# Three of the eight input tiles transposed on VectorE, by way of DRAM, during the convolution's first unit

## The chip, the cores and the metric
The kernel runs on one core of a Trainium2 chip. The metric is the time on the device of one execution, in microseconds (us). The core has five engines with a queue of instructions each: TensorE (PE, products and transposes through its array), VectorE (DVE), ScalarE (ACT), GpSimd (POOL) and SyncE (SP, which here only issues transfers). They run side by side and are tied together by semaphores: an instruction waits until a counter has reached a value and adds to a counter when it is done.

## What is computed
One decoder block on x of 1024 tokens by 1024 channels, in float32. The part that matters here is its beginning:

```python
h = rmsnorm(x, g_mix[i])
z = h @ w_in[i]                       # 1024 x 1536
a = z[..., :C_CONV]; b = z[..., C_CONV:2 * C_CONV]; v = z[..., 2 * C_CONV:]
u = a * jax.nn.sigmoid(b)
u = causal_depthwise_conv(u, conv_w[i], conv_b[i])      # 31 taps, 512 channels
u = jax.nn.silu(layernorm(u, ln_g[i], ln_b[i]))
q = multiscale_pool(v, pool_w[i], pool_scale[i])
x = x + jnp.concatenate([u, q], axis=-1) @ w_out[i]
# then a SwiGLU FFN, a gated per-token embedding and a final rmsnorm
```

## The kernel before
**Precision and tiles.** Each float32 operand of a product is split into a rounded high part and a low part (hi and lo); one product is three matmuls (lo x hi, hi x lo, hi x hi: L1659 to L1661). ScalarE writes the high part (`copy`, L1042), VectorE or GpSimd the low part as source minus high part (`lo`, L2035 and L788). Tokens lie in eight tiles of 128 (t = 0 to 7), channels in eight blocks of 128 (k).

**The input side.** For each tile: SP loads x into `xres[:, t]` (the tile `resid`), ScalarE sums its squares (`square_x`), GpSimd makes the factor (`rms`), VectorE multiplies by it and by the gain (`normed`, L2063) into one of two slots of `scr`, TensorE transposes the 8 blocks of 128x128 into two banks of PSUM (`turn`, L1708), ScalarE copies them to `act_hi` (`turned_hi`) and VectorE makes `act_lo` from them (`turned_lo`), in two halves each.

**The products.** TensorE computes a and b in eight products n = 0 to 7, ordered by `AB`: n = 0 to 3 are the channel groups for tokens 0 to 511, n = 4 to 7 those for tokens 512 to 1023. Each is two halves (a, then b) of 24 matmuls of 128x512, in two banks of PSUM: 0 and 1 for even n, 2 and 3 for odd n. Product 0 is done in pieces while the first tiles come in. Product 1 needs weight stripes 2 and 3 (`ws_lo`), products 2 and 3 those of `bs_hi` and `bs_lo`: stripes 0 and 1, whose low parts VectorE makes, and 2 and 3, whose low parts GpSimd makes. Products 4 to 7 need `act_lo` of all eight tiles. Tiles 4 and 5 are transposed between the pieces of product 0, 6 and 7 between the halves of product 1. `evac_ab` on ScalarE moves a product out, GpSimd multiplies by the gate (`gate_u`).

**The convolution.** It runs on VectorE in eight units of 31 taps (`convolve`, L2129), one for each group of 128 channels and half of the tokens. The first `OWN` taps of a unit are made by ScalarE (`first_taps`, L1094) and summed by GpSimd (`sum_taps`), 2 in units 0 and 7. VectorE's first two taps of a unit read two operands in SBUF, the later ones accumulate in PSUM. `between` names steps that are set in after a tap of a given number: in unit 1 the two transposes of p (`turn_p`), later layer norm and the low parts of the mixing. GpSimd waits at some places until VectorE has done the first two taps of a unit (`unit_begun`), not for unit 7.

**Behind it.** The v part of the projection, a product for e, the pooled products (each waits for the low part of the one before, `q_low`), the output projection for each tile, and a second norm whose tiles 0 to 4 already go the way that the change takes: stored to DRAM, loaded in runs of 32 elements, transposed on VectorE (`store_xn`, `load_xn`, `block_turn`, L2215). The latter needs the end of unit 7, because the same queue of VectorE holds the additions (`add_x`, L2181) behind it.

**What sets the order.** It is written by hand: each engine's program is a list of calls, and an engine never passes one that waits. DMA queues go in the order in which SP issues them.

Of the kernel before, what the change touches and what calls it, by code (L numbers as in the profile page):

```python
# [39 lines left out]
def hybrid_block(nc, x, p, g_mix, w_in, conv_w, conv_b, ln_g, ln_b, pool_w, pool_scale, w_out,  # L40
# [34 lines left out]
    xg_dram = nc.dram_tensor("xg_scratch", (TT, 2, P, BANK), F32, kind="Internal").ap()  # L75
    x1_dram = nc.dram_tensor("x1_scratch", (TT, P, D), F32, kind="Internal").ap()
    in_dram = nc.dram_tensor("in_scratch", (7, PAIRS, P, BANK), F32, kind="Internal").ap()

    with ExitStack() as ctx:
# [79 lines left out]
        def turns(n):  # L159

            by_dve = sum(TT <= k < TT + MIX_TILES or 0 <= k - 2 * TT and k - 2 * TT in DVE_TURNS for k in range(n))
            return 2 * (n - by_dve)

        DVE_TURNS = (0, 1, 2, 4, 6)

# [48 lines left out]
        xn_turned = sem("xn_turned")  # L214
        w_hi = sem("w_hi")
# [125 lines left out]
        def turn_bank(norm, t):  # L341

            return (6 - 2 * (t % 2), 4 * (t % 2), 2 if t % 2 == 0 else 0 if t == 1 else 4)[norm]
# [199 lines left out]
        def _(sp):  # L543
# [234 lines left out]
        def _(pool):  # L778
# [261 lines left out]
        def _(act):  # L1040
# [86 lines left out]
            turned_hi(4, 0)  # L1127
            turned_hi(5, 0)
# [527 lines left out]
        def _(pe):  # L1656
# [30 lines left out]
            def turn(t, norm):  # L1687
                n = norm * TT + t
                for j in range(2):
# [67 lines left out]
            turn(4, 0)  # L1757
            turn(5, 0)
# [9 lines left out]
            for n in range(1, 2 * KC):  # L1768
# [33 lines left out]
            for s in range(GROUPS):  # L1802
                pe.wait_ge(w_lo, S_V + s + 1)
# [35 lines left out]
            pe.wait_ge(w_lo, S_PLE + KP)  # L1839
# [779 lines left out]
```

## Time and profile before

| | |
|---|---|
| Time, median of 3 runs | 992.76 us (992.42 to 993.64) |
| Profiled execution: its own time | 994.86 us |
| Profiled execution: its span | 992.9 us |
| TensorE busy | 980.3 us (99%) |
| VectorE busy | 710.7 us (72%) |
| ScalarE busy | 458.1 us (46%) |
| GpSimd busy | 380.4 us (38%) |
| Clock granted to TensorE | 0.998 of full, on average |

The span is the time from the first to the last instruction in one profiled execution; the times are of executions without the profiler. The matmuls' ends are modelled, so small waits of TensorE are seen better in the distance between starts than in its busy time. Of two engines that are busy at once only the one on which the other waits counts for the end.

### The profile page before, as it was taken

The page shows a single profiled execution, that of the slowest core. Times are in us where ns is not written, and L with a number is a line of the kernel's source. Part 1 is how long each engine was busy: PE and PEld are TensorE (multiplying, and loading weights), DVE is VectorE, ACT ScalarE, POOL GpSimd, SP SyncE. Part 2 cuts the span into 40 slices and gives each one's busy share as a digit, 9 for nine tenths or more (in the row PEclk, how much of TensorE's full clock was granted, in tenths as well). Part 3 has the DMA queues.
Part 4 walks back from the last instruction along what each step waited for, and adds up shares of the span by engine and source line. Part 5 has one row for each costly group of instructions (what it writes and reads, how often), then busy time and mean ns, then how long its engine had stood idle before and what let it go on. Part 6 is the DMA issues. An engine that isn't in the chain of part 4 may idle for free.

```text
span 992.9 us, 12311 instructions
## 1 busy us (share of the span) xinstructions
PE 980.3 (99%) x4447; PEld 812.3 (82%) x4447; DVE 710.7 (72%) x982; ACT 458.1 (46%) x704; POOL 380.4 (38%) x288
## 2 busy tenths in 40 slices
PE   9999999999999999999999999999999999999996
PEld 7888888888788888888888888888888888888885
DVE  6899999996798355354454544553677888887897
ACT  7625347404363333423333333333444665676865
POOL 3445889710245544444354353442000000012555
PEclk9999999999999999999999999999999999999999
DMA  7620112558724234233332432412999788657432
GB/s 257 140 87 40 45 41 116 202 172 190 211 64 153 60 109 121 89 107 95 117 107 80 133 107 64 148 64 99 355 370 322 233 304 268 198 159 201 152 107 106
DMA packets 154799, 148.74 MB, mean 150 GB/s; under 512 B 56507, under 2 KB 110291, under 8 KB 154739
## 3 DMA queue, kind: packets, MB, share of 16 engines
q1 hardware_dynamic: 153536, 147.56, 46.7%
q8 instruction: 35, 0.57, 0.2%
q10 hardware_dynamic: 1202, 0.40, 0.2%
q14 instruction: 26, 0.20, 0.1%
HBM read 109.92 MB, written 38.01 MB: 149 GB/s over the span
## 4 chain that ended last, share of the span: by engine, by line
PE 70%; DVE 2%; DMA 2%; SPq 1%; issue 1%; POOL 1%; ACT 1%; POOLq 0%; DVEq 0%; ACTq 0%
PE ps L1659 23%; PE ps L1661 23%; PE ps L1660 23%; SPq L627 1%; DMA xn_scratch<-scr 1%; DMA scr<-xn_scratch 1%; PE ps L1708 0%; DVE resid L2181 0%; DVE scr L2063 0%; DVE ftmp L2522 0%; POOL rs L785 0%; DVE resid L2525 0%; DVE act_lo L2035 0%; SPq L632 0%; ACT junk L1056 0%
## 5 line engine op out<-in xcount | busy, mean ns | idle before, releaser
L782 POOL TENSOR_SCALAR ss<-ss 128x1 f32<-128x1 f32 x38 | 14.5, 381 | 322.0 <-ACT junk L1056 286.6
L2129 DVE SCALAR_TENSOR_TENSOR ps<-resid,convw,ps 128x512 f32<-128x512 f32 x190 | 127.4, 749 | 0.0
L1659 PE MATMUL ps<-ring_hi,ring_lo 128*128 128x512 f32 x308 | 119.9, 389 | 0.1
L1661 PE MATMUL ps<-ring_hi 128*128 128x512 f32 x308 | 119.8, 389 | 0.0
L1660 PE MATMUL ps<-ring_lo,ring_hi 128*128 128x512 f32 x308 | 119.8, 389 | 0.0
L1659 PE MATMUL ps<-act_hi,bs_lo 128*128 128x512 f32 x240 | 93.5, 389 | 0.0
L1660 PE MATMUL ps<-act_lo,bs_hi 128*128 128x512 f32 x240 | 93.4, 389 | 0.0
L1661 PE MATMUL ps<-act_hi,bs_hi 128*128 128x512 f32 x240 | 93.4, 389 | 0.0
L2288 DVE TENSOR_TENSOR gtmp<-ps,gtmp 128x512 f32<-128x512 f32 x22 | 15.2, 691 | 95.6 <-PE ps L1661 95.6
L1042 ACT ACTIVATE ring_hi<-raw 128x512 fp32r<-128x512 f32 x89 | 51.9, 625 | 60.5 <-PE ps L1661 58.1
L2035 DVE TENSOR_TENSOR ring_lo<-raw,ring_hi 128x512 fp32r<-128x512 f32 x89 | 58.0, 688 | 22.9 <-ACT ring_hi L1042 22.8
L788 POOL TENSOR_TENSOR wc_lo<-raw_b,wc_hi 128x1024 fp32r<-128x1024 f32 x22 | 55.6, 2525 | 48.9 <-ACT wc_hi L1042 47.8
L1659 PEld LDWEIGHTS ps<-ring_hi,ring_lo 128*128 128x128 f32 x308 | 57.8, 188 | 12.3 <-DVE ring_lo L2035 0.5
L1661 PEld LDWEIGHTS ps<-ring_hi 128*128 128x128 f32 x308 | 57.8, 188 | 12.1
L1660 PEld LDWEIGHTS ps<-ring_lo,ring_hi 128*128 128x128 f32 x308 | 57.8, 188 | 12.0
L788 POOL TENSOR_TENSOR bs_lo<-raw_b,bs_hi 128x1024 fp32r<-128x1024 f32 x24 | 58.0, 2417 | 23.0 <-ACT bs_hi L1042 14.7
L788 POOL TENSOR_TENSOR bs_lo<-raw,bs_hi 128x1024 fp32r<-128x1024 f32 x17 | 41.1, 2425 | 62.6 <-ACT bs_hi L1042 62.6
L1659 PE MATMUL ps<-act_hi,ws_lo 128*128 128x512 f32 (+1 forms) x144 | 53.5, 372 | 0.3 <-DVE act_lo L2035 0.2
L1659 PEld LDWEIGHTS ps<-act_hi,bs_lo 128*128 128x128 f32 x240 | 45.1, 188 | 9.4
L1661 PEld LDWEIGHTS ps<-act_hi,bs_hi 128*128 128x128 f32 x240 | 45.1, 188 | 9.4
L1661 PE MATMUL ps<-act_hi,ws_hi 128*128 128x512 f32 (+1 forms) x144 | 52.7, 366 | 0.0
L1660 PE MATMUL ps<-act_lo,ws_hi 128*128 128x512 f32 (+1 forms) x144 | 52.7, 366 | 0.0
(281 smaller groups left out, 2620.7 us busy)
## 6 DMA issues: line engine op xcount, KB each, us to landing
raw<-in_w_gate_up SPq DMA_DIRECT2D x44, 512.0 KB, 5.2
raw<-in_scratch SPq DMA_DIRECT2D x52, 256.0 KB, 3.3
raw<-in_w_down SPq DMA_DIRECT2D x52, 256.0 KB, 4.2
in_scratch<-in_s SPq DMA_DIRECT2D x44, 256.0 KB, 3.4
in_scratch<-gtmp SPq DMA_DIRECT2D x33, 256.0 KB, 2.3
keep<-in_w_down SPq DMA_DIRECT2D x32, 256.0 KB, 4.1
keep<-in_scratch SPq DMA_DIRECT2D x25, 256.0 KB, 3.6
resid<-in_x SPq DMA_DIRECT2D x8, 512.0 KB, 6.9
```

The lines of the kernel that those rows point to most:

```text
L627: sp.dma_start(xn_place(TT + t)[a * SQ:(a + 1) * SQ, :].rearrange("j (k b i) -> j k b i", k=KD, i=SQ), src)\
L782: pool.tensor_scalar(ss[:, n:n + 1], ss[:, n:n + 1], 1.0 / D, EPS, ALU.mult, ALU.add)\
L788: pool.tensor_tensor(dst, src, hi.bitcast(F32), ALU.subtract).then_inc(done, 1)
L1042: act.activation(dst, src, ACT.Copy, scale=scale).then_inc(done, 1)
L1659: pe.matmul(dst, w_lo_, m_hi, start=start, stop=False, skip_group_check=onto)
L1660: pe.matmul(dst, w_hi_, m_lo, start=False, stop=False, skip_group_check=onto)
L1661: return pe.matmul(dst, w_hi_, m_hi, start=False, stop=stop, skip_group_check=onto)
L2035: dve.tensor_tensor(dst, src, hi.bitcast(F32), ALU.subtract).then_inc(done, 1)
L2129: dve.scalar_tensor_tensor(out=conv_c if k == last_odd else acc, in0=u_all[:, c, k + h * BANK:k + (h + 1) * BANK], scalar=convw[:, c * 32 ...
L2288: dve.tensor_tensor(gtmp[:, 3, :], ps[:, X_BANK[q % 2], :], gtmp[:, 3, :], ALU.add).then_inc(c22_ok, 1)
```

## The change
**Which tiles.** Tiles 4, 5 and 6 (`X_DVE`) are normed in place, into `xres[:, t]` and not into `scr`. SP stores each to DRAM (`xa_scratch`, `store_xa`) and loads it again with four DMAs (`load_xa`), each for 32 partitions and in runs of 32 elements, so that the 32x32 blocks stand where a transposition by blocks needs them. VectorE then transposes the 128x1024 in one instruction into banks 6 and 7 (`x_turn`). Tile 7 is still transposed by TensorE, between the halves of product 1, now into banks 0 and 1, which product 2 uses next. `act_hi` and `act_lo` are made as before, in the order of tiles 7, 4, 5, 6 (`x_place`).

**What moves.** TensorE loses 24 transposes. The three block transposes, four `turned_lo` and the low part of stripe 1 of bs are set in between the taps of units 0 and 1. ScalarE makes the first taps of unit 0 before it copies stripe 1. GpSimd does the first two v stripes before those for e, so TensorE's counts of `w_lo` change with it. The stores and loads come ahead of the loads of p in SP's queue.

The diff, in the order SP, GpSimd, ScalarE, TensorE, VectorE behind the tables of numbers:

```diff
         def turns(n):
-            by_dve = sum(TT <= k < TT + MIX_TILES or 0 <= k - 2 * TT and k - 2 * TT in DVE_TURNS for k in range(n))
+            by_dve = sum(k in X_DVE or TT <= k < TT + MIX_TILES or 0 <= k - 2 * TT and k - 2 * TT in DVE_TURNS for k in range(n))
...
+        X_DVE = (4, 5, 6)
+        def x_place(t):
+            return t if t < 4 else 4 if t == 7 else t + 1
...
         def turn_bank(norm, t):
-            return (6 - 2 * (t % 2), 4 * (t % 2), 2 if t % 2 == 0 else 0 if t == 1 else 4)[norm]
+            return ((6, 4, 6, 4, 6, 6, 6, 0)[t], 4 * (t % 2), 2 if t % 2 == 0 else 0 if t == 1 else 4)[norm]
...
+            def store_xa(t):
+                sp.wait_ge(xn_ok, t + 1)
+                sp.dma_start(xa_dram[t - 4], x_tile(t, 0)).then_inc(xa_moved[t - 4], DMA)
+            def load_xa(t):
+                sp.wait_ge(xa_moved[t - 4], DMA)
+                for a in range(P // SQ):
+                    src = xa_dram[t - 4].rearrange("(b j) (k a i) -> a j k b i", j=SQ, a=P // SQ, i=SQ)[a]
+                    sp.dma_start(x_tile(t, 0)[a * SQ:(a + 1) * SQ, :].rearrange("j (k b i) -> j k b i", k=KD, i=SQ), src)\
+                      .then_inc(xa_moved[t - 4], DMA)
...
             unit_begun(3)
-            for r in range(KP):
-                split_row(raw_b, r, bs_hi[:, 2 + r, :], bs_lo[:, 2 + r, :], S_PLE + r + 1)
             gate_u(6)
             for s in range(2):
                 split_cols(V_STRIPE[s], S_V + s + 1, at=s)
+            split_row(raw_b, 0, bs_hi[:, 2, :], bs_lo[:, 2, :], S_PLE + 1)
+            gate_u(7)
             sum_taps(KC)
-            gate_u(7)
+            split_row(raw_b, 1, bs_hi[:, 3, :], bs_lo[:, 3, :], S_PLE + 2)
...
-            turned_hi(4, 0)
-            turned_hi(5, 0)
             square_x(6)
             square_x(7)
             evac_ab(0)
-            for m in range(2):
-                split_cols(m, 2 * DMA, bs_hi)
-            turned_hi(6, 0)
+            split_cols(0, 2 * DMA, bs_hi)
+            first_taps(0)
+            split_cols(1, 2 * DMA, bs_hi)
             turned_hi(7, 0)
-            first_taps(0)
             evac_ab(1)
...
+            turned_hi(4, 0)
             first_taps(1)
+            turned_hi(5, 0)
             evac_ab(2)
+            turned_hi(6, 0)
...
-            turn(4, 0)
-            turn(5, 0)
...
+                if n == 2:
+                    pe.wait_ge(act_lo_ok, 2 * x_place(7) + 2)
                 if n == KC:
                     pe.wait_ge(act_lo_ok, 2 * TT)
                 ab_part(n, 0)
                 if n == 1:
-                    turn(6, 0)
                     turn(7, 0)
...
-            turned_lo(4, 0)
-            turned_lo(5, 0)
             normed(6, 0, 1)
             normed(7, 0, 1)
...
+            def x_turn(t):
+                dve.wait_ge(xa_moved[t - 4], DMA * (1 + P // SQ))
+                dve.wait_ge(act_lo_ok, 2 * x_place(t))
+                dve.transpose(ps[:, 6:8, :].rearrange("p b n -> p (b n)"), x_tile(t, 0)).then_inc(xa_turned, 1)
+            b_stripe_low(0)
+            dve.wait_ge(act_lo_ok, 2 * HT)
...
-            convolve(0, {})
-            convolve(1, {8: lambda: turn_p(0), 16: lambda: turn_p(1)})
+            convolve(0, {2: lambda: b_stripe_low(1), 4: lambda: turned_lo(7, 0), 8: lambda: x_turn(4),
+                         12: lambda: turned_lo(4, 0), 16: lambda: x_turn(5), 20: lambda: turned_lo(5, 0),
+                         25: lambda: x_turn(6)})
+            convolve(1, {0: lambda: turned_lo(6, 0), 8: lambda: turn_p(0), 16: lambda: turn_p(1)})
```

VectorE's queue from the constants (`qscale`) to unit 0, before. The rows L2035 are `act_lo` of tiles 4 and 5, then two stripes of `bs_lo`, then `act_lo` of 6 and 7; L2129 are taps.

```order
L2035 TENSOR_TENSOR act_lo<-ps,act_hi 128x4x128 [waits act_hi_ok] x4
L2063 SCALAR_TENSOR_TENSOR scr<-resid,rs,gain 128x1024 [waits turned,rs_ok] x2
L2035 TENSOR_TENSOR bs_lo<-raw,bs_hi 128x1024 [waits w_hi] x2
L2035 TENSOR_TENSOR act_lo<-ps,act_hi 128x4x128 [waits act_hi_ok] x4
L2129 SCALAR_TENSOR_TENSOR ps<-resid,convw,gain 128x512 [waits taps_in,act_lo_ok]
L2129 SCALAR_TENSOR_TENSOR ps<-resid,convw,gain 128x512
L2129 SCALAR_TENSOR_TENSOR ps<-resid,convw,ps 128x512 [waits taps_done] x25
```

The same place now (the lines are 31 to 35 further down): L2094 are the norms of tiles 6 and 7, L2164 taps, L2140 the transpose of tile 4.

```order
L2094 SCALAR_TENSOR_TENSOR resid<-resid,rs,gain 128x1024 [waits rs_ok]
L2094 SCALAR_TENSOR_TENSOR scr<-resid,rs,gain 128x1024 [waits turned,rs_ok]
L2066 TENSOR_TENSOR bs_lo<-raw,bs_hi 128x1024 [waits w_hi]
L2164 SCALAR_TENSOR_TENSOR ps<-resid,convw,gain 128x512 [waits taps_in,act_lo_ok]
L2164 SCALAR_TENSOR_TENSOR ps<-resid,convw,gain 128x512
L2164 SCALAR_TENSOR_TENSOR ps<-resid,convw,ps 128x512 [waits taps_done]
L2066 TENSOR_TENSOR bs_lo<-raw,bs_hi 128x1024 [waits w_hi]
L2164 SCALAR_TENSOR_TENSOR ps<-resid,convw,ps 128x512 [waits taps_done] x2
L2066 TENSOR_TENSOR act_lo<-ps,act_hi 128x4x128 [waits act_hi_ok] x2
L2164 SCALAR_TENSOR_TENSOR ps<-resid,convw,ps 128x512 [waits taps_done] x4
L2140 STREAM_TRANSPOSE ps<-resid 128x1024 [waits act_lo_ok,xa_moved0]
L2164 SCALAR_TENSOR_TENSOR ps<-resid,convw,ps 128x512 [waits taps_done] x4
```

Everything that came between the norms and the taps but the first stripe now stands behind taps; four taps on there follow `act_lo` of tile 4, the transpose of 5, and so on.

SP's queue from the last weights of product 1 to p, before: L550 are stripes of w_in, L587 the loads of p.

```order
L562 DMA resid<-in_x 128x1024 x2
L550 DMA raw<-in_w_in 128x8x256 [waits w_lo]
L550 DMA raw<-in_w_in 128x8x256
L587 DMA raw_b<-in_p 32x32x32 x8
L589 DMA pw_raw<-in_pool_w 128x4x128
```

And now: L594 are the stores, L600 the loads of tiles 4, 5 and 6, L614 those of p.

```order
L571 DMA resid<-in_x 128x1024 x2
L594 DMA xa_scratch<-resid 128x1024 [waits xn_ok] x2
L559 DMA raw<-in_w_in 128x8x256 [waits w_lo]
L559 DMA raw<-in_w_in 128x8x256
L600 DMA resid<-xa_scratch 32x32x32 [waits xa_moved0]
L600 DMA resid<-xa_scratch 32x32x32 x3
L594 DMA xa_scratch<-resid 128x1024 [waits xn_ok]
L600 DMA resid<-xa_scratch 32x32x32 [waits xa_moved1]
L600 DMA resid<-xa_scratch 32x32x32 x3
L600 DMA resid<-xa_scratch 32x32x32 [waits xa_moved2]
L600 DMA resid<-xa_scratch 32x32x32 x3
L614 DMA raw_b<-in_p 32x32x32 x8
```

Two stores stand ahead of the stripes, a third store and twelve loads between them and p.

## Rows read from the trace of the kernel before
In a timeline a row is: start us, us in all, engine, line, operation, output <- inputs, shape, how many in a row, and in brackets the idle time before it and what ended it. In the view of a line: duration in ns (min/median/max), first and last start in us; then the time from a DMA's issue to its landing.

**Rows 1.** Timeline, TensorE, around its waits at 250, 261 and 271 us.
```profile
249.49 0.39 PE L1661 MATMUL ps<-bs_hi,act_hi 128*128 128x512 f32 x1
250.02 0.50 PE L1659 MATMUL ps<-bs_hi,act_lo 128*128 128x512 f32 x1
...
260.81 0.39 PE L1661 MATMUL ps<-ws_hi,act_hi 128*128 128x512 f32 x1
261.25 1.09 PE L1708 MATMUL ps<-ident,scr 128*128 128x128 f32 x8
...
270.14 0.39 PE L1661 MATMUL ps<-bs_hi,act_hi 128*128 128x512 f32 x1
271.49 1.09 PE L1708 MATMUL ps<-ident,scr 128*128 128x128 f32 x8 [0.95 <-DVE scr L2063]
```

**Rows 2.** Timeline, TensorE: transposes of tiles 4 and 5; what follows; start of product 2.
```profile
22.68 1.91 PE L1708 MATMUL ps<-ident,scr 128*128 128x128 f32 x16
24.52 0.43 PE L1763 MATMUL ps<-ident,scr 31*128 31x31 f32 x4
...
40.58 0.39 PE L1659 MATMUL ps<-act_hi,bs_lo 128*128 128x512 f32 x1
```

**Rows 3.** Timeline, VectorE, 31 to 65 us: low parts, unit 0, start of unit 1.
```profile
31.98 1.23 DVE L2035 TENSOR_TENSOR bs_lo<-raw,bs_hi 128x1024 fp32r<-128x1024 f32 x1 [0.87 <-ACT bs_hi L1042]
35.36 1.23 DVE L2035 TENSOR_TENSOR bs_lo<-raw,bs_hi 128x1024 fp32r<-128x1024 f32 x1 [2.16 <-ACT bs_hi L1042]
36.51 2.48 DVE L2035 TENSOR_TENSOR act_lo<-ps,act_hi 128x512 fp32r<-128x512 f32 x4
39.02 1.43 DVE L2129 SCALAR_TENSOR_TENSOR ps<-resid,convw,gain 128x512 f32<-128x512 f32 x2
40.35 16.55 DVE L2129 SCALAR_TENSOR_TENSOR ps<-resid,convw,ps 128x512 f32<-128x512 f32 x25
...
59.05 1.42 DVE L2129 SCALAR_TENSOR_TENSOR ps<-resid,convw,gain 128x512 f32<-128x512 f32 x2
...
64.99 1.24 DVE L2195 STREAM_TRANSPOSE wide<-raw_b 128x1024 f32<-128x1024 f32 x1
```

**Rows 4.** Timeline, ScalarE: copy of stripe 1, first taps, evacuation of product 3.
```profile
34.27 1.06 ACT L1042 ACTIVATE bs_hi<-raw 128x1024 fp32r<-128x1024 f32 x1 [2.33 <-DMA raw<-in_w_in]
...
37.14 0.83 ACT L1094 ACTIVATE gain<-resid,cvec,convw 128x512 f32<-128x512 f32 x1
37.85 0.73 ACT L1094 ACTIVATE gain<-resid,convw 128x512 f32<-128x512 f32 x1
...
62.54 0.60 ACT L1077 ACTIVATE resid<-ps 128x512 f32<-128x512 f32 x1 [9.79 <-PE ps L1661]
```

**Rows 5.** View of line L587, the loads of p: all eight, and the last.
```profile
L587 SPq DMA_DIRECT2D raw_b<-in_p x8: 563/970/3202, 26.7 to 38.0; - x8
...
L587 SPq DMA_DIRECT2D raw_b<-in_p x1: 902/902/902, 38.0 to 38.0; - x1
...
DMA to landing us min/median/max: 4.5/4.5/4.5
```

**Rows 6.** Timeline, VectorE and GpSimd, first steps of unit 6.
```profile
160.82 1.29 DVE L2035 TENSOR_TENSOR act_lo<-ps,act_hi 128x512 fp32r<-128x512 f32 x2 [0.61 <-ACT act_hi L1042]
...
169.50 1.28 DVE L2169 SCALAR_TENSOR_TENSOR act_lo<-ps,qscale,act_hi 128x1024 fp32r<-128x1024 f32 x1 [0.80 <-ACT act_hi L1042]
...
160.38 2.41 POOL L903 TENSOR_TENSOR scr<-wide,scr 128x1024 f32<-128x1024 f32 x1 [1.78 <-DVE ps L2129]
```

**Rows 7.** Timeline, VectorE and GpSimd, first taps of unit 7.
```profile
186.31 5.59 DVE L2129 SCALAR_TENSOR_TENSOR ps<-resid,convw,gain 128x512 f32<-128x512 f32 x2
...
186.14 5.20 POOL L788 TENSOR_TENSOR bs_lo<-raw,bs_hi 128x1024 fp32r<-128x1024 f32 x2 [0.54 <-ACT bs_hi L1042]
```

**Rows 8.** Timeline, VectorE, 226 to 230 us.
```profile
226.39 0.69 DVE L2181 TENSOR_TENSOR resid<-ps,raw_b 128x512 f32<-128x512 f32 x1 [0.98 <-PE ps L1661]
229.00 1.25 DVE L2215 STREAM_TRANSPOSE raw<-scr 128x1024 f32<-128x1024 f32 x1 [1.92 <-DMA scr<-xn_scratch]
```

More of the change, by code:

```diff
@@ L75, in hybrid_block @@
     xg_dram = nc.dram_tensor("xg_scratch", (TT, 2, P, BANK), F32, kind="Internal").ap()
+    xa_dram = nc.dram_tensor("xa_scratch", (3, P, D), F32, kind="Internal").ap()
     x1_dram = nc.dram_tensor("x1_scratch", (TT, P, D), F32, kind="Internal").ap()
@@ L214, in hybrid_block @@
         xn_turned = sem("xn_turned")
+        xa_moved = [sem(f"xa_moved{j}") for j in range(3)]
+        xa_turned = sem("xa_turned")
         w_hi = sem("w_hi")
@@ L581, in _ @@
             load_x(7, xres[:, 7, :])
+            def store_xa(t):
[7 more added lines that the diff above has]
+                      .then_inc(xa_moved[t - 4], DMA)
+            store_xa(4)
+            store_xa(5)
             sp.wait_ge(w_lo, S_B)
             load_cols(w_in_v, 256, C + 256)
+            load_xa(4)
+            store_xa(6)
+            load_xa(5)
+            load_xa(6)
             for k in range(KP):
@@ L1060, in turned_hi @@
                 for j in range(2):
-                    act.wait_ge(turned, 2 * n + j + 1)
+                    if n in X_DVE:
+                        act.wait_ge(xa_turned, X_DVE.index(n) + 1)
+                    else:
+                        act.wait_ge(turned, turns(n) + j + 1)
                     copy(act_hi[:, 4 * j:4 * j + 4, t * P:(t + 1) * P],
@@ L1693, in turn @@
                         pe.wait_ge(xn_ok, n + 1)
-                    if norm == 0 and t >= 2:
+                    if norm == 0 and 2 <= t < 4:
                         pe.wait_ge(act_lo_ok, 2 * n + j - 3)
+                    if norm == 0 and t == 7:
+                        pe.wait_ge(ab_ev, 1)
                     if norm == 1 and t >= HT_MIX + 2:
@@ L1802, in _ @@
             for s in range(GROUPS):
-                pe.wait_ge(w_lo, S_V + s + 1)
+                pe.wait_ge(w_lo, S_V + s + 1 - (KP if s < 2 else 0))
                 if s < 2:
@@ L1838, in _ @@
             pe.wait_ge(p_lo_ok, KP)
-            pe.wait_ge(w_lo, S_PLE + KP)
+            pe.wait_ge(w_lo, S_PLE + KP + 2)
             for t in range(TT):
@@ L2037, in turned_lo @@
             def turned_lo(t, norm, halves=range(2)):
-                n = t if norm == 0 else TT + t
+                n = x_place(t) if norm == 0 else TT + t
                 for j in halves:
@@ L2057, in normed @@
                         dve.wait_ge(xn_turned, n - TT - 1)
-                    else:
+                    elif n not in X_DVE:
                         dve.wait_ge(turned, turns(n - 1))
@@ L2062, in normed @@
                         dve.wait_ge(gain_ok, 2)
-                    ins = dve.scalar_tensor_tensor(out=xn_place(n)[:, c], in0=x_tile(t, norm)[:, c], scalar=rs[:, n:n + 1],
+                    ins = dve.scalar_tensor_tensor(out=(x_tile(t, norm) if n in X_DVE else xn_place(n))[:, c], in0=x_tile(t, norm)[:, c], scalar=rs[:, n:n + 1],
                                                    in1=pair(2)[:, c] if n < 5 else gain[:, c],
@@ L2098, in _, with b_stripe_low @@
             ins.then_inc(const_ok, 1)
-            turned_lo(4, 0)
-            turned_lo(5, 0)
             normed(6, 0, 1)
             normed(7, 0, 1)
-            for m in range(2):
+            def b_stripe_low(m):
                 dve.wait_ge(w_hi, S_B + m + 1)
                 lo(cols_stripe(bs_lo, m), cols_of(raw, m), cols_stripe(bs_hi, m), w_lo)
-            turned_lo(6, 0)
-            turned_lo(7, 0)
-            dve.wait_ge(act_lo_ok, 2 * TT)
+            def x_turn(t):
[4 more added lines that the diff above has]
+            dve.wait_ge(act_lo_ok, 2 * HT)
             even, odd = ps[:, 4, :], ps[:, 5, :]
```

## The prediction, made before the change was timed

> **What bounds the kernel now.** I read the page first: TensorE is busy for 980.3 us of 992.9, so only work on TensorE, or a wait of TensorE, can move the end. Then the waits of TensorE: it waits at very few places. The ones near this change lie at 250, 261 and 271 us: the gaps between starts are 0.53, 0.44 and 1.35 us where 0.23 is the rule, so 0.3, 0.2 and 1.1 us, 1.6 in all [rows 1]. Then the timelines of the first 65 us, since the change lies there, and of 155 to 272 us, to see who TensorE waits for later. There TensorE waits for a chain of VectorE and DMA which begins when VectorE ends the eight convolution units. So two clocks matter: how much TensorE moves (call it s) and how much the convolution's end moves (call it c).
>
> **Removed from TensorE.** 24 transposes (tiles 4, 5, 6). Sixteen hold TensorE from 22.68 to 24.52 us, 0.115 each [rows 2], so 24 of them 2.76 us. All of it is on TensorE's path. Without other waits product 2 of the input projection (counted from 0; the first that reads bs_lo) would start at 40.58 - 2.8 = 37.8 us.
>
> **The convolution begins sooner.** What it needs is on ScalarE: the copy of stripe 0 of bs, after which VectorE starts its own part at 31.98 [rows 3], and then the first two taps, which took 37.14 to 38.58 [rows 4], 1.44 us. Now the taps stand right behind stripe 0, so unit 0 starts at about 31.9 + 1.4 = 33.3 us where it was 39.02 [rows 3]. The copy of stripe 0 waits for its transfer, which is issued at the same point as before; the two stores put ahead of it in SP's queue wait only for norms that VectorE has done before the stripe on which that transfer waits, so I take no delay.
>
> **What now stands inside unit 0.** Taps come every 0.66 us (25 in 16.55 us), a bs_lo stripe costs 1.15, one tile's two act_lo halves 2 x 0.63 = 1.25 (four in 2.5) [rows 3], and a VectorE transpose of 128x1024 1.17 (64.99 to the next tap) [rows 3]. In order:
> - three taps to 35.3; stripe 1 of bs_lo needs ScalarE's copy, which waits for its transfer until 34.27 and ends at 35.33 [rows 4]: to 36.5; two taps to 37.8; act_lo of tile 7 to 39.15. **First stall:** product 2 now waits for this one (its bank held tile 7). It starts at 39.2, not 37.8: 1.4 us lost, still 1.4 ahead of before.
> - four taps, transpose of tile 4 (41.7 to 42.9), four taps, act_lo of tile 4, four taps, transpose of tile 5 (49.4), four taps, act_lo of 5, five taps, transpose of 6 (57.8), three taps and the end of the unit. Unit 1 starts at 61.8 (before: 59.05 [rows 3]); one tap, then act_lo of tile 6, done at 63.8.
> - **Second stall:** product 4 needs act_lo of all tiles. Products 2 and 3 took from 40.58 [rows 2] to 62.35 (ScalarE's evacuation at 62.54 [rows 4] follows by 0.2), 21.8 us. So TensorE is ready at 39.2 + 21.8 = 61.0 and waits until 63.85: 2.9 us lost. TensorE is now 1.5 us **later** than before (63.85 against 62.35), and VectorE 4.0 later (61.8 + 1.25 against 59.05).
>
> In sum: removed -2.8, waits +1.4 and +2.9. The three transposes (3.5 us) went from an engine with no slack to one whose result that engine needs, and VectorE's idle time ahead of unit 0, for which they might have been filled in, is still there.
>
> **The transfers.** The new loads have the shape of those of p: 128 KB in runs of 32 elements. Those eight were issued from 26.7 to 38.0 and the last landed 4.5 later, at 42.5 [rows 5], behind two stripes that landed by 34.3 [rows 4]: 1.0 us each. The four of tile 4 take the place of the first four, so they land at 38.4, for a transpose at 41.7: 3.3 us spare. Store 6, tile 5 (44), tile 6 (48 to 49) and then p (57, needed at 69) have more. I take nothing for them; without this cover each us of lateness above the slack costs one.
> The Trainium skill (VectorE: DVE Perf Modes, The three transpose paths) says that a plain DMA that does the transposing by strides is 19 times slower than the crossbar's, and (DMA: Bandwidth & Descriptors, Specifications) that pieces under 512 B miss line rate. That speaks against the change: by it the tiles would come tens of us late. The rows of p show about 4 us for a tile in such runs, and the sum goes by them.
>
> **From there to 190 us.** s = 1.5, VectorE +4.0. Units 1 to 3 have no waits to give back. VectorE's idle 0.61 before act_lo of the mixing (160.82) is used up, and 0.4 ahead of it, so it comes 3.0 late to the first pooled product's low part, and had waited 0.80 there (169.50) [rows 6]: that step ends 2.2 later than before. TensorE waits for it before the next pooled product, so s grows to 2.2. GpSimd waited at 160.38 for unit 6's second tap [rows 6], so its chain comes 3.7 late, ScalarE waits for that and delays the second pooled product's evacuation by 0.6 more: s = 2.8. Bounds: 1.5 if this slack is wider than I read it, 3.3 if ScalarE comes one step later. I take 2.8.
>
> **The end of the convolution.** Unit 7 starts when the last of these products is through: 186.31 + 2.8 = 189.1. Before, its first two taps took 5.59 us and not 1.42, while GpSimd's two bs_lo stripes ran from 186.14 to 191.34 [rows 7]. Each tap was held for one GpSimd instruction, 2.1 us. Now GpSimd starts these stripes about 3.6 later (189.8): the first tap is clear by 0.7 and the second on the edge. So c = 2.8 - 2.1 or 2.8 - 4.2: +0.7 or -1.4.
> (The Trainium skill, SBUF - State Buffer, SBUF: two separate sides, calls this an exclusive lock for a whole instruction between GpSimd and a VectorE instruction with two SBUF inputs. By that rule the price comes in whole steps, where a shared rate would give something between; the row, two taps of about 2.8, agrees with the lock.)
>
> **Where the delay is paid back.** VectorE's addition at 226.39 waited for TensorE [rows 8], so it comes at 229.2; the first block transpose (229.00, it waited for its transfer) then starts at 229.9: the chain moves by 0.9, whichever of the two c holds. At 271.49 TensorE needs that chain at +0.9, and would itself be ready at +2.8 - 1.6 (its old waits [rows 1]) = +1.2. The later counts: **+1.2 us** at 272, and no wait behind it that would absorb or add.
>
> **The sum.** The profiled execution's span is 992.9 us: -2.8 +1.4 +2.9 +1.3 (pooling part) -1.6 (old waits) = +1.2, so 994.1. Its own time was 994.86, above the runs' median of 992.76; I put the difference on the median: **994.0**. A measurement of this kernel tells 0.2% (2.0 us) from no change, so this is "no change".
>
> **Rivals.**
> 1. The pooling part has more slack (s stays about 1.5) and unit 7 is free of GpSimd. Then TensorE is at 1.5 - 1.6, the chain below zero: 992.7. For: three of my links there have less than 0.7 us of margin. Chance 0.15.
> 2. **Slower: both first taps of unit 7 meet GpSimd again.** c = +2.8, all of the chain to 271 moves by it and TensorE waits for it: 995.6. It decides when GpSimd starts the stripes before 189.1, 0.7 sooner than I place it (or unit 7 is 0.7 later). For: it is what happens before. Chance 0.20.
> 3. Slower: the runs of 32 land late. At twice p's 1.0 us the four of tile 4 land at 34.3 + 8.3 = 42.6, 0.9 after their transpose is due; the store of tile 6 takes its turn (1.5, half of a 1 MB stripe's 2.9 to 3.3) and tile 5 lands at 52.4, 2.2 after its own shifted turn; tile 6 is then in time. Product 4 comes 3.1 later still: 997.0. It decides from a tile 4 later than 41.7. Against: the rows of p. Chance 0.06.
> 4. Faster: product 4 is not waited for, because VectorE is quicker or TensorE's need later than I think. Then -2.8, and of the 1.6 of waits up to all: 988.5 to 990.5, say 990. Against: it takes 2.9 us off a row of steps of known length. Chance 0.09.
> My forecast has 0.50.
>
> **Numbers.** Rivals 1 and the forecast lie within 0.2%: 0.65; 2 and 3 are slower: 0.26; 4 is faster: 0.09. Range: from 1 to 2 with the bounds of s and some spread of the runs (992.42 to 993.64): 991.9 to 996.2; 4 and most of 3 are left out.
>
> **What would show it.** TensorE: product 2 at 39.2 and product 4 at 63.8, each after a wait for VectorE's act_lo, 1.4 and 2.9 us; unit 0 starting at 33.3; transposes on VectorE at 41.7, 49.4 and 57.8 with no wait for DMA; unit 1 at 61.8; unit 7 at 189.1 with one long tap or none; the turn before 272 at 272.6. I am wrong if product 4 starts before 62.3, if a transpose waits for its loads, or if unit 7's taps are both long.

## The result, and the profile after

| | us, median | lowest to highest | profiled execution | its span |
|---|---|---|---|---|
| before | 992.87 | 992.42 to 994.18 | 994.86 | 992.9 |
| after | 996.10 | 995.26 to 998.45 | 995.38 | 993.5 |

The ratio after to before is 1.0033, 95% interval 1.0024 to 1.0042: slower, by 3.2 us. The time lies at the upper edge of the range, beyond the forecast of 994.0.

The two profiled spans differ by 0.6 us only, because the profiled execution of before lay 2.1 us above its kernel's median. The first experiment below gives a second profile of it, near the median (992.62, span 990.7), and "before" in what follows is that one. Every trace has its own zero: one and the same piece of product 0 starts anywhere from 19.4 to 20.3 us (19.53 in before, 19.41 in after). I write s for how much later than there TensorE is, and v for the same of VectorE; both hold this difference of zeros unless it is named.

The views that answer to those of before. Waits of TensorE in the changed kernel, whole span (engine, line, waited for: us in total, times, longest):

```profile
PE ps L1689 <- DVE act_lo L2066: 3.7, 4, 2.3
```

Its timeline at the second of these waits, where product 4 starts:

```profile
60.55 0.39 PE L1691 MATMUL ps<-act_hi,bs_hi 128*128 128x512 f32 x1
63.25 0.50 PE L1689 MATMUL ps<-act_hi,bs_lo 128*128 128x512 f32 x1 [2.31 <-DVE act_lo L2066]
63.55 0.62 PE L1690 MATMUL ps<-act_lo,bs_hi 128*128 128x512 f32 x1
63.97 0.63 PE L1691 MATMUL ps<-act_hi,bs_hi 128*128 128x512 f32 x1
...
66.53 0.59 PE L1691 MATMUL ps<-act_hi,bs_hi 128*128 128x512 f32 x1
66.96 0.40 PE L1689 MATMUL ps<-act_hi,bs_lo 128*128 128x512 f32 x1
67.20 0.39 PE L1690 MATMUL ps<-act_lo,bs_hi 128*128 128x512 f32 x1
```

From 63.55 to 66.96 us eight steps are 0.43 us apart; before the wait and after 66.96 they are 0.23 apart. The view of stretches says the same (stretch, its length, busy time and count of PE, PEld, DVE, ACT and POOL, the granted clock, DMA share, GB/s):

```profile
61.00:63.25 2.25, 0.00 (x1) 0.04 (x1) 2.15 (x5) 1.06 (x2) 0.00 (x0) 1.00 0.00 0
63.25:67.00 3.75, 3.75 (x10) 2.93 (x11) 3.75 (x7) 3.20 (x6) 1.29 (x1) 0.54 0.02 4
67.00:75.00 8.00, 8.00 (x37) 6.61 (x36) 8.00 (x13) 0.69 (x2) 4.81 (x2) 1.00 0.00 0
```

The granted clock is 0.54: nearly the whole stretch at the lower level, 1.2 GHz, right after an idle time of 2.3 us. That costs 8 x 0.20 = 1.6 us, and no term of the prediction had it. The Trainium skill (TensorE: Matmul & The Clock Gate, What's actually happening) describes these two levels and says that activity releases the higher one; the rows show both levels, and TensorE at work when the higher one comes back.

VectorE at the steps that replace [rows 3] and [rows 7]: the transposes wait for nothing, `act_lo` of tile 6 stands in unit 1, and both first taps of unit 7 are long again:

```profile
41.30 1.25 DVE L2140 STREAM_TRANSPOSE ps<-resid 128x1024 f32<-128x1024 f32 x1
48.88 1.25 DVE L2140 STREAM_TRANSPOSE ps<-resid 128x1024 f32<-128x1024 f32 x1
57.13 1.25 DVE L2140 STREAM_TRANSPOSE ps<-resid 128x1024 f32<-128x1024 f32 x1
61.15 0.76 DVE L2164 SCALAR_TENSOR_TENSOR ps<-resid,convw,gain 128x512 f32<-128x512 f32 x1
61.82 1.28 DVE L2066 TENSOR_TENSOR act_lo<-ps,act_hi 128x512 fp32r<-128x512 f32 x2
...
115.98 0.69 DVE L2172 TENSOR_TENSOR resid<-ps,resid 128x512 f32<-128x512 f32 x1
...
188.75 5.64 DVE L2164 SCALAR_TENSOR_TENSOR ps<-resid,convw,gain 128x512 f32<-128x512 f32 x2
```

So where did 3.2 us come from? TensorE's first transposes of the convolution's output start at 119.35 us, 116.62 before: s = 2.7 there, and it stays 2.7 through its transposes at 272.11 (269.39 before) to the end (2.8 there: span 993.5 against 990.7). The other 0.4 of the 3.2 us is not in these two traces. All of the loss is made in the first 67 us: -2.7 for the 24 transposes, +1.15 and +2.5 for the two waits, +1.6 for the clock are 2.5 of the 2.7.

### The profile page after: what moved, and what is told of

Read it like the earlier page. It is cut to its first block, busy times and chain, and to the rows that moved or that the text cites. A ratio compares the mean times of both kernels' runs of the same rounds, so it can differ in the third digit from the quotient of the medians.

```text
span 993.5 us, 12276 instructions
## 1 busy us (share of the span) xinstructions
PE 978.8 (99%) x4423; PEld 810.8 (82%) x4423; DVE 713.4 (72%) x985; ACT 458.5 (46%) x704; POOL 382.3 (38%) x288
## 4 chain that ended last, share of the span: by engine, by line
PE 92%; DVE 5%; issue 1%; DMA 1%; ACT 1%; POOL 0%; POOLq 0%; DVEq 0%; ACTq 0%
PE ps L1689 30%; PE ps L1691 30%; PE ps L1690 30%; DVE ps L2164 2%; DVE act_lo L2066 1%; PE ps L1740 1%; DMA raw<-in_w_in 1%; DMA resid<-in_x 0%; DVE ftmp L2559 0%; PE ps L1829 0%; PE ps L1819 0%; DVE ps L2140 0%; DVE ws_lo L2066 0%; DVE resid L2562 0%; POOL rs L812 0%
## 5 line engine op out<-in xcount | busy, mean ns | idle before, releaser
L809 POOL TENSOR_SCALAR ss<-ss 128x1 f32<-128x1 f32 x38 | 16.9, 444 | 317.3 <-ACT junk L1083 281.9
L2164 DVE SCALAR_TENSOR_TENSOR ps<-resid,convw,ps 128x512 f32<-128x512 f32 x190 | 127.8, 746 | 0.0
L1689 PEld LDWEIGHTS ps<-ring_hi,ring_lo 128*128 128x128 f32 x308 | 57.8, 188 | 12.3 <-DVE ring_lo L2066 0.5
L1690 PEld LDWEIGHTS ps<-ring_lo,ring_hi 128*128 128x128 f32 x308 | 57.8, 188 | 12.1
L1691 PEld LDWEIGHTS ps<-ring_hi 128*128 128x128 f32 x308 | 57.8, 188 | 12.0
L1690 PEld LDWEIGHTS ps<-act_lo,bs_hi 128*128 128x128 f32 x240 | 45.3, 189 | 9.4
```

The lines of the kernel that those rows point to most:

```text
L809: pool.tensor_scalar(ss[:, n:n + 1], ss[:, n:n + 1], 1.0 / D, EPS, ALU.mult, ALU.add)\
L1689: pe.matmul(dst, w_lo_, m_hi, start=start, stop=False, skip_group_check=onto)
L1690: pe.matmul(dst, w_hi_, m_lo, start=False, stop=False, skip_group_check=onto)
L1691: return pe.matmul(dst, w_hi_, m_hi, start=False, stop=stop, skip_group_check=onto)
L2164: dve.scalar_tensor_tensor(out=conv_c if k == last_odd else acc, in0=u_all[:, c, k + h * BANK:k + (h + 1) * BANK], scalar=convw[:, c * 32 ...
```

## The experiments

Each time stands beside its ratio to before, with the 95% interval. Before was timed anew beside each group of runs: 992.95 beside runs 1 to 4, 993.26 beside 5 to 8, 993.39 beside 9 to 11, 993.30 beside 12. Times of different groups are better compared by their ratios.

**1. The kernel before again.** No edit.

> The kernel before, unchanged, for a second profile. Theory A (TensorE's position decides; the three waits of TensorE at 250, 261 and 271 us, 1.6 us in all, belong to the one execution that was profiled, which was 2.0 us above the median): the time is 992.9 within 0.4, and in an execution near the median these waits are under 0.5 us in all. Theory B (the waits belong to the kernel, and VectorE's chain decides at 271): they are there again, 1.3 to 1.9 us in all, in an execution near the median too.

Measured: 992.73, ratio 0.9997 (0.9988 to 1.0006). TensorE's waits in it, whole span, and VectorE's block transposes that stand ahead of them:

```profile
PE ps L1715 <- POOL ident L803: 1.6, 1, 1.6
PE ps L1659 <- DVE act_lo L2035: 0.2, 1, 0.2
PE ps L1708 <- DVE scr L2063: 0.2, 1, 0.2
```

```profile
243.37 1.25 DVE L2215 STREAM_TRANSPOSE raw<-scr 128x1024 f32<-128x1024 f32 x1 [2.14 <-DMA scr<-xn_scratch]
250.63 1.25 DVE L2215 STREAM_TRANSPOSE raw<-scr 128x1024 f32<-128x1024 f32 x1 [2.82 <-DMA scr<-xn_scratch]
262.23 1.26 DVE L2215 STREAM_TRANSPOSE ps<-scr 128x1024 f32<-128x1024 f32 x1 [1.00 <-DMA scr<-xn_scratch]
```

The waits of [rows 1] are gone. In the profile that I had read, the third of these transposes, started by its transfer, came at 264.38, and TensorE at 271.49 instead of 269.39: 2.1 us, all that the execution had above the median. Theory A holds: the 1.6 us came from late transfers of that execution and are no slack that the kernel always has. Executions so far above the median are not rare (three of the sixteen beside runs 1 to 4 took 994.27 to 994.43), but whether for the same cause no trace shows.

**2. GpSimd out of the way of unit 7.**

```diff
                 wo_q(j)
+            unit_begun(7)
             for j, k in enumerate((2, 3, 0, 1)):
```

> The changed kernel with one added wait: GpSimd starts its four bs_lo stripes only when VectorE has done the first two taps of unit 7. Both theories: these two taps take 1.4 us instead of 5.6, and the convolution ends 4.2 us sooner (208.6 instead of 212.8). Theory A: TensorE never waits for that end in the changed kernel, so the time stays at 996.1 within 0.5. Theory B, rival 2 of the prediction (VectorE's chain sets TensorE at 271): the chain and the time come 2 to 3 us sooner, 993.1 to 994.1.

Measured: 996.12, ratio 1.0031 (1.0019 to 1.0043). The two taps took 1.4 us, not 5.6, the convolution ends sooner, and VectorE then waits 3.80 us for TensorE before an addition (last row), where it waited 0.57 in the changed kernel:

```profile
188.85 1.43 DVE L2165 SCALAR_TENSOR_TENSOR ps<-resid,convw,gain 128x512 f32<-128x512 f32 x2
190.19 16.56 DVE L2165 SCALAR_TENSOR_TENSOR ps<-resid,convw,ps 128x512 f32<-128x512 f32 x25
208.09 0.69 DVE L2173 TENSOR_TENSOR resid<-ps,resid 128x512 f32<-128x512 f32 x1
...
228.91 0.69 DVE L2217 TENSOR_TENSOR resid<-ps,raw_b 128x512 f32<-128x512 f32 x1 [3.80 <-PE ps L1692]
```

The convolution ends 4.1 us sooner than in the changed kernel and the time does not move: this collision costs nothing. (In runs 3, 4, 5 and 7 it did not come about either, the two taps took 1.42 to 1.43 us, and none of them is the faster for it.) The same trace holds a second case of the clock. Here stripe 1 arrived late, the first wait was 1.84 us long, and eight slow steps followed it:

```profile
39.67 0.47 PE L1690 MATMUL ps<-act_hi,bs_lo 128*128 128x512 f32 x1 [1.84 <-DVE act_lo L2067]
39.97 0.47 PE L1691 MATMUL ps<-act_lo,bs_hi 128*128 128x512 f32 x1
40.24 0.63 PE L1692 MATMUL ps<-act_hi,bs_hi 128*128 128x512 f32 x1
40.67 0.63 PE L1690 MATMUL ps<-act_hi,bs_lo 128*128 128x512 f32 x1
```

**3 and 4. The second wait taken away, then both.**

```diff
-... 25: lambda: x_turn(6)})
-convolve(1, {0: lambda: turned_lo(6, 0), 8: ...
+... 21: lambda: x_turn(6), 24: lambda: turned_lo(6, 0)})
+convolve(1, {8: ...
```

In 4 also `turned_lo(7, 0)` directly after `b_stripe_low(1)`, and after taps 15, 19, 20 and 23 the steps `x_turn(5)`, `turned_lo(5, 0)`, `x_turn(6)`, `turned_lo(6, 0)`.

> The changed kernel with VectorE's transpose of tile 6 after tap 21 and its act_lo after tap 24 of unit 0 (they stood after tap 25 and in unit 1). act_lo is done at 59.0 and product 4 is ready at 60.8, so the wait of 2.5 us is gone. Theory A with the clock (after this wait TensorE ran at 1.2 GHz for 8 steps of 0.43 us instead of 0.23, and that is the wait's doing): 2.5 + 1.6 = 4.1 sooner than the changed kernel, 992.0, and no stretch at half clock. Without a link between wait and clock: 2.5 sooner, 993.6, and the half clock is still there. If VectorE's chain decides later on: less than 2 us sooner, over 994.

> As the run before it, and act_lo of tile 7 directly behind stripe 1 of bs_lo (two taps sooner), the steps of tiles 5 and 6 one more tap sooner. act_lo of tile 7 is done at 37.4, product 2 is ready at 37.7: the first wait (1.15 us) is gone too. Theory A: 990.9, 2.0 sooner than the kernel before, TensorE 2.6 ahead of it from product 2 on. Theory B (the chain at 271 or VectorE elsewhere takes over once TensorE is sooner): TensorE waits at 250 to 272 for what it gained, 992 to 993.

Measured: 996.63, ratio 1.0035 (1.0022 to 1.0047), and 997.52, ratio 1.0045 (1.0032 to 1.0059). Neither gained anything, against theory A in both; what is left is that something later decides. The second wait and the slow steps are gone in both, but others have come. TensorE's waits in run 3:

```profile
PE ps L1689 <- DVE act_lo L2066: 1.8, 3, 1.4
...
PE ps L1819 <- DVE resid L2172: 1.2, 1, 1.2
PE ps L1740 <- DVE scr L2094: 0.7, 1, 0.7
PE ps L1689 <- DVE act_lo L2204: 0.5, 1, 0.5
```

L2172 is the end of unit 3, on which TensorE's transposes at 117 us now wait, and L2204 the low part of a pooled product, before the second of these products (Q2, counted from 0 the third). In VectorE's and TensorE's timelines of run 3:

```profile
116.36 0.69 DVE L2172 TENSOR_TENSOR resid<-ps,resid 128x512 f32<-128x512 f32 x1
...
117.11 1.09 PE L1819 MATMUL ps<-ident,resid 128*128 128x128 f32 x8 [1.16 <-DVE resid L2172]
...
177.28 0.47 PE L1689 MATMUL ps<-ws_hi,act_lo 128*128 128x512 f32 x1 [0.53 <-DVE act_lo L2204]
```

With the end of unit 3 and the start of Q2 read from the traces, a rule appears (us; "before" is its second profile, the numbers are those of the runs, before and behind this place):

| kernel | unit 3 ends | Q2 starts | between | waits at Q2 |
|---|---|---|---|---|
| before (run 1) | 113.05 | 174.89 | 61.84 | no |
| after | 116.67 | 177.62 | 60.95 | no |
| 2 | 117.47 | 177.70 | 60.23 | yes |
| 3 | 117.05 | 177.28 | 60.23 | yes |
| 4 | 118.13 | 178.36 | 60.23 | yes |
| 5 | 117.10 | 177.88 | 60.78 | no |
| 6 | 113.99 | 174.24 | 60.25 | yes |
| 7 | 116.24 | 176.47 | 60.23 | yes |
| 8 | 118.59 | 178.82 | 60.23 | yes |
| 9 | 112.61 | 174.00 | 61.39 | no |
| 10 | 117.01 | 178.79 | 61.78 | no |
| 11 | 113.55 | 175.25 | 61.70 | no |
| 12 | 117.73 | 177.98 | 60.25 | yes |

Where TensorE waits, Q2 starts 60.2 us after VectorE's unit 3, to 0.02, and in no trace is it sooner. Before, VectorE had 1.6 us of slack there; the change makes it 3.6 later. So TensorE cannot be better than s = 3.6 - 1.6 = 2.0 at Q2, whatever happens in the first 67 us. In the changed kernel its own 2.7 covers this bound up. The bound is not the last one: in run 3 TensorE is at s = 2.4 at Q2, a little ahead of the changed kernel, but its trace adds 0.9 at 272.67 us, behind a block transpose that had waited 1.91 us for its transfer, and 0.6 more by 924 us. The trace of the changed kernel has neither.

**5 and 12. TensorE kept busy while it waits.** The identity times itself, into the bank that product 4 overwrites; run 12 has 9 in place of 18.

```diff
                 if n == KC:
+                    keep_warm(18)
                     pe.wait_ge(act_lo_ok, 2 * TT)
```

> The changed kernel with 18 extra 128x128 products of the identity on TensorE (into the bank that product 4 overwrites) ahead of the wait before product 4. They fill about 2 us of the 2.5 that TensorE idles there. Theory C (a wait of about 1.8 us or more on TensorE is followed by a stretch at 1.2 GHz, 8 steps of 0.43 us instead of 0.23, 1.6 us): there is no such stretch after product 4 starts, and TensorE is 1.1 behind the kernel before at 100 us, not 2.7, as long as the first wait stays under 1.5 us. Rival (the low clock comes from something else in the chip at that moment): the stretch is there all the same. The end gains less than 1.6 in either case, since VectorE's unit 3, over at 116.7 to 117.0, holds TensorE at 117 us to at least 0.4 behind: 995.0 to 996.0 by C, 996.1 by the rival.

> As e5_busy_while_waiting with 9 extra products instead of 18: the 18 took 3.9 us and outlasted the wait (product 4 started at 65.1 us, 1.6 later than act_lo allowed), 9 take 2.0 and should end inside it. Theory C (a longer wait of TensorE brings the stretch at 1.2 GHz): product 4 starts at 63.3 to 63.6, all its steps are 0.23 us apart, and TensorE is 1.2 to 1.4 behind the kernel before at its transposes near 118 us (after: 2.7). VectorE is as late as in the changed kernel, so TensorE is held at its second pooled product to 2.0 to 2.4 behind: the time is 995.4 to 996. Rival: the slow stretch is there with its 1.6 us all the same, 996.1.

Measured: 996.38, ratio 1.0029 (1.0019 to 1.0040), and 995.95, ratio 1.0024 (1.0013 to 1.0034). TensorE in run 12; the steps behind the second row are 0.23 us apart to the end of the stage, as in run 5:

```profile
39.94 0.47 PE L1689 MATMUL ps<-act_hi,bs_lo 128*128 128x512 f32 x1 [1.57 <-DVE act_lo L2067]
...
61.81 2.17 PE L1747 MATMUL ps<-ident 128*128 128x128 f32 x18
```

(The trace has two records for each of the nine products.)

No slow steps in either: the low clock behind the wait at 63 us hangs on TensorE's standing idle in it, and not on something else at that moment. That is one execution each, and the length of the wait alone does not decide: in run 10 below no slow steps follow an idle time of 2.65 us. In run 12 product 4 starts at 64.20, not at 63.3 to 63.6, and TensorE is at s = 2.1 at 118.74 us, of which 0.4 is this trace's later zero, where 1.2 to 1.4 was expected; VectorE was later in it too (unit 3 at 117.73). Then the bound of the table takes it back: Q2 starts at 177.98, 60.25 after unit 3. The time is that of the changed kernel within the error. In run 5 the filler outlasted the wait and cost TensorE 1.6 us; its time says nothing about the clock.

**6. The transposes on VectorE made short.** Run 4 with 32 of 1024 columns in each; the rest of the transposing is left out.

```diff
-dve.transpose(ps[:, 6:8, :].rearrange(...), x_tile(t, 0))
+dve.transpose(ps[:, 6, 0:SQ], x_tile(t, 0)[:, 0:SQ])
```

> The run without the two early stalls (e4_no_stalls, 997.5), where each of VectorE's three transposes handles 32 of the 1024 columns: part of the input's transposing is left out, all waits, loads and stores are as they were. VectorE is some 3.2 us sooner. Theory D (VectorE has become the bound: its unit 3 ends 3.8 us later than before where the slack ahead of TensorE's transposes at 116.6 is 3.5): the waits of TensorE at 117, 129 and 177 us vanish or shrink under 0.3 in all, and the time is 990.4, 2.5 below the kernel before. Rival E (the extra DMA traffic or the new order of steps costs the time): 995 or more, with the waits still there.

Measured: 993.31, ratio 0.9998 (0.9989 to 1.0007). The transposes' time on VectorE is thus worth 4.2 us of run 4's 997.5 (4.7 by the ratios), and the stores, loads and new order do not by themselves make the kernel slower than before. But the 2.5 below before did not come either. TensorE is 2.4 ahead at 114.24 us (116.62 before) and meets VectorE's statistics step at 126 (0.5), a copy of ScalarE at 157 (0.6) and Q2 (0.6), where the rule holds it, since VectorE's unit 3 still ends 0.9 later than before. It is 0.7 ahead at 277.80 (278.48), and in this execution loses that and 0.8 more from 917 us on, behind a transfer for which VectorE waits 3.45 us (1.51 before).

**7, 8 and 9. Fewer tiles through VectorE.** Run 4 with tiles 5 and 6 (7) or tile 6 alone (8, 9) on the new path, the others transposed by TensorE as before. In 9 ScalarE copies tile 6 ahead of product 2's evacuation:

```diff
-            evac_ab(2)
             turned_hi(6, 0)
+            evac_ab(2)
             evac_ab(3)
```

> As e4_no_stalls, but tile 4 goes through TensorE's transposes again, as before the change (its act_lo in VectorE's idle time ahead of 31.7 us); tiles 5 and 6 stay on VectorE. TensorE saves 1.84 us instead of 2.76; VectorE's unit 1 starts at 60.0, 1.2 later than before instead of 3.8. Theory D: no wait at 117 or 129, TensorE 1.8 ahead at 130; about 1.2 of it is lost at 177 or at 250 to 272, where VectorE's chain is 1.2 late: 991.1 to 992.3. Rival E: 994 or more.

> Only tile 6 goes through DRAM and VectorE; tiles 4 and 5 are transposed on TensorE. TensorE saves 0.92 us. VectorE pays 1.17 for one transpose and gains the 2.1 us that it idled ahead of unit 0: about 1 us sooner than before. Theory D: no wait of TensorE on VectorE after 40 us, 0.9 ahead all the way: 992.0. Rival E: 993.5 or more.

> Tile 6 alone through DRAM and VectorE, as in e8_tile_6_only, where VectorE idled 5.3 us in unit 0 because ScalarE's copy of tile 6 stood behind the evacuation of product 2. Here the copy stands ahead of it, and act_lo comes four taps later. The law read from the runs so far (theory F): with v how much later than in the kernel before VectorE's unit 3 ends, and s how much later TensorE is, TensorE's second pooled product after 174.9 us starts at s = v - 1.6 or at TensorE's own s, whichever is later. Here v is about -0.5 and TensorE's own s -0.9: s = -0.9, 992.2, and no wait of TensorE for VectorE from 40 to 200 us. Rival (the DRAM detour itself costs): 994 or more.

Measured: 994.43, ratio 1.0010 (1.0001 to 1.0019); 996.32, ratio 1.0029 (1.0018 to 1.0040); 993.15, ratio 1.0000 (0.9991 to 1.0009). All three missed what was expected. Run 7's time is in the range of rival E, but run 6 speaks against E, and run 7's trace shows VectorE later than the 1.2 expected: unit 3 ends at 116.24, 3.2 later than before (0.8 of it this trace's later zero), and TensorE waits for VectorE at 116, 129 and 176 us, 0.5 each. Run 8 missed by an oversight of mine, which VectorE's timeline shows:

```profile
44.96 2.69 DVE L2164 SCALAR_TENSOR_TENSOR ps<-resid,convw,ps 128x512 f32<-128x512 f32 x4
52.91 1.29 DVE L2064 TENSOR_TENSOR act_lo<-ps,act_hi 128x512 fp32r<-128x512 f32 x2 [5.26 <-ACT act_hi L1065]
```

VectorE stood still for 5.3 us within unit 0, since ScalarE's queue held tile 6's copy behind an evacuation that had to wait for product 2. Again VectorE's lateness, and no work of TensorE's, made the time. Mended in run 9, VectorE is 0.4 ahead of before (112.61) and TensorE 0.9 ahead from 116 us (115.74) to 278, without a wait on VectorE between 40 and 200 us. As a whole time that is 993.15 against 993.39: no version tried beats the kernel before by more than the measurement tells.

**10 and 11. Each half of the change alone, on the kernel before.** Run 11 leaves out 18 of 24 transposes, so part of the input's transposing is not done.

```diff
-            convolve(0, {})
+            convolve(0, {8: extra_turn, 16: extra_turn, 25: extra_turn})
```

```diff
-                    for q in range(4):
+                    for q in range(3 if norm == 0 and t in (4, 5, 6) else 0, 4):
```

> The kernel before with three transposes of 128x1024 added on VectorE in unit 0, into banks that nobody reads: the change's load on VectorE alone. Theory F: v = +3.5; TensorE waits nothing or 0.1 at 117 us, 0.7 in all at 129 and 1.9 at Q2 (starts at 176.8 instead of 174.9), so 994.9. Rival G (VectorE has room for it, and only TensorE's own early waits cost the changed kernel its time): 993.0 within 0.4.

> The kernel before with 18 of the 24 transposes of tiles 4, 5 and 6 left out (the last of each four stands), so part of the input's transposing is not done: the change's relief of TensorE alone, 18 x 0.115 = 2.1 us. The prediction's view (TensorE's time is the kernel's time): 2.1 sooner all the way, 990.8. Theory F: v is 0 or slightly below (unit 0 waits for a copy of tile 7 that comes a little sooner), TensorE is held at Q2 to s = -1.6 at the soonest: 991.3, with waits of 0.5 in all between 126 and 178 us. If still other chains hold it (DMA at 229 to 272, as in the run with short transposes): 992 to 993.

Measured: 997.45, ratio 1.0040 (1.0028 to 1.0053), and 993.18, ratio 1.0002 (0.9993 to 1.0011). Three transposes on VectorE alone cost 4 us, more than the rule said, and 18 fewer on TensorE alone bring nothing. Both go back to one place, which the rule did not hold. TensorE at its V products in run 10, then in run 11:

```profile
109.42 0.50 PE L1659 MATMUL ps<-act_hi,ws_lo 128*128 128x512 f32 x1 [2.65 <-POOL ws_lo L788]
109.75 0.40 PE L1660 MATMUL ps<-act_lo,ws_hi 128*128 128x512 f32 x1
109.98 0.39 PE L1661 MATMUL ps<-act_hi,ws_hi 128*128 128x512 f32 x1
```

```profile
105.96 0.50 PE L1659 MATMUL ps<-act_hi,ws_lo 128*128 128x512 f32 x1 [1.35 <-POOL ws_lo L788]
```

And GpSimd before and in run 10:

```profile
97.26 4.79 POOL L788 TENSOR_TENSOR bs_lo<-raw_b,bs_hi 128x1024 fp32r<-128x1024 f32 x2 [4.92 <-DVE ps L2129]
101.98 1.12 POOL L833 TENSOR_TENSOR resid<-resid,wide 128x512 f32<-128x512 f32 x1
103.03 4.79 POOL L788 TENSOR_TENSOR ws_lo<-raw,ws_hi 128x1024 fp32r<-128x1024 f32 x2
```

```profile
101.22 4.78 POOL L788 TENSOR_TENSOR bs_lo<-raw_b,bs_hi 128x1024 fp32r<-128x1024 f32 x2 [4.94 <-DVE ps L2129]
105.95 1.10 POOL L833 TENSOR_TENSOR resid<-resid,wide 128x512 f32<-128x512 f32 x1
107.00 2.37 POOL L788 TENSOR_TENSOR ws_lo<-raw,ws_hi 128x1024 fp32r<-128x1024 f32 x1
```

GpSimd begins the split of `raw_b` only when VectorE has begun unit 3, and the V stripes stand behind it. A VectorE that is 4.0 late (0.8 of it is run 10's later zero) makes the stripes 4.0 late, and TensorE needs the first as it is done. In run 11 TensorE comes to this place 1.3 ahead and leaves it 0.2 behind. The rows of run 10 also bear on the clock: this wait of 2.65 us is TensorE's longest in any trace here, longer than the 2.31 that was followed by slow steps, and the steps behind it are 0.23 us apart.

The changed kernel escapes the late stripes by an edit whose worth I had passed over: on GpSimd the V stripes stand ahead of these splits.

## Why the prediction was right, and where it was not

The range held the time, at its upper end; the forecast itself, no change, did not come: 0.33% is above the 0.2% that I had set. By the prediction's steps:

- **Removed.** 2.8 forecast. Product 2 would have started at 38.89 - 1.15 = 37.74, 40.46 before: 2.7. Right.
- **The convolution sooner, and what stands in it.** Unit 0 at 33.3 forecast, 33.02 measured; transposes at 41.7, 49.4 and 57.8 against 41.30, 48.88 and 57.13, none waiting for its transfer; unit 1 at 61.8 against 61.15. VectorE 4.0 later forecast, 3.6 measured. Right.
- **The waits.** 1.4 and 2.9 forecast, 1.15 and 2.5 measured. Right, but the step took a wait to cost its own length. With these waits alone TensorE would have been 1.0 late where the forecast had 1.5; the missing term is the clock, +1.6 in this trace, which makes it the 2.7 measured. Not all of the 1.6 counts for the time: without it the bound at Q2 would have held TensorE to 2.0, and run 12, which has no slow steps, is no faster than the error tells.
- **The transfers.** Nothing forecast for them, and run 6 bears it out. The Trainium skill (VectorE: DVE Perf Modes, The three transpose paths) gives its factor of 19, against the crossbar's transpose, for a plain DMA whose innermost destination stride is large. The prediction left this condition out, and these loads do not meet it: they write runs of 32 elements side by side and leave the transposing inside the blocks to VectorE. The twelve loads landed 3.0 to 8.0 us after their issue, ahead of every transpose.
- **From there to 190 us.** s was to grow by 1.3 and did not grow. What limits TensorE there is the later of its own place and unit 3's end + 60.2. With 1.5 of its own it would have been pulled to 2.0; with 2.7 it was beyond. That TensorE waits there for VectorE was right, as runs 2, 3 and 12 show; the size was not, and the part of it that was put down to ScalarE's evacuation no run tests.
- **The end of the convolution.** Here a step failed: GpSimd started its stripes at 188.63, not 189.8, and both taps were held (5.64 us), as rival 2 said. But run 2 shows that rival 2's price was wrong too: nothing waits for c.
- **Where the delay is paid back.** This step failed. I took 1.6 us of waits, from [rows 1], as slack that a later TensorE absorbs. They were gone in a second execution, near the median (run 1). I had noted that this execution was 2.1 us above the median, and set that difference aside in the last line instead of asking which rows carried it. Both were the same 2 us: counted as slack in the sum, then taken off again as a difference.

With the clock in, no growth and nothing paid back, the same sum is -2.7 + 1.15 + 2.5 + 1.6 = 2.5 on the median of 992.9, 995.4; the measured TensorE shift of 2.7 gives 995.6, against 996.1; the last 0.5 stays unexplained. That the range held is luck: it held because the omissions (1.6 of clock and 1.6 of payback that never came) were partly met by the 1.3 of growth that did not come, and because rival 2 had drawn its upper end, by a mechanism that was not at work.

What neither forecast nor rivals had: the change could not have paid even without the waits. VectorE's 3.5 us more of work were set against 1.6 us of slack, and steps of ScalarE (run 6) and GpSimd (run 11) hold TensorE too once it gains more than about 0.7 us. "TensorE is busy 980 of 993 us" is true, and yet four engines are due at nearly the same moments.

Run 4 is not faster than run 3, although it has one early wait fewer. In its trace the pieces of product 0 start 0.7 later and VectorE idles 0.60 us more, for ScalarE's copy of stripe 1; unit 3 ends 1.1 later, and by the rule Q2 starts 1.1 later too. Whether other executions are like these, one profile of each cannot tell.

What stays open: the late transfer near 917 us is not run 6's alone. Between 917 and 925 us TensorE loses 0.6 to 1.4 us in the traces of runs 3, 4, 6, 7 and 11, and at most 0.2 in the others, before and after among them. No run shows what makes that transfer late.

## What to carry to other kernels

An engine that is busy 99% of the time and waits nowhere may still have no slack under it: look not for its waits but for how long its inputs had been ready, since that is all that work moved to their engine may take. Before a wait is counted as slack, see it in a second execution, above all when the profiled one is as far above the median as the wait is long. And look at the steps behind a wait of TensorE, not only at its length: of three idle times of 1.84 to 2.65 us two were followed by 1.6 us of slow steps and the longest was not.

## What the runs showed of the hardware

- Idle times of TensorE of 2.31 and 1.84 us were each followed by eight steps at 1.2 GHz, 0.43 us each, 1.6 us in all (after, run 2). Idle times of 1.00, 1.35, 1.39 and 1.57 us (after, runs 5, 3, 12) were not, nor was the wait at 63 us when it was filled with small products (runs 5 and 12), nor an idle time of 2.65 us (run 10). So length alone does not decide, and what does these runs do not tell.
- Two VectorE taps that meet GpSimd's stripes took 5.59 us in the first trace of before, 5.43 in the second and 5.64 after, and 1.43 when kept apart (run 2): 2.0 to 2.1 more for each tap (5.27 to 5.40 in runs 9, 10 and 11). It comes in whole steps: in runs 6, 8 and 12 one tap only was held, and the two took 3.58, 3.59 and 3.62 us; no trace has a sum between 1.43 and 3.58 or between 3.62 and 5.27.
- In run 10 the granted clock reads 0.95 in every stretch, while the steps of TensorE are 0.23 us apart as in all others; its later end is TensorE's later place at 282.74 us (278.48 before) alone.
